# Second block of a two-block transformer kernel: norm weight in the rounding pass, deviation at the PSUM reads, last panels finished tile by tile

## The chip, the cores and the metric

One core of a Trainium2 chip runs the whole program. The metric is the device time of one execution in microseconds, the median of several runs; smaller is better. Before the change the median is 3257.94 us over three runs (3250.87 to 3266.14).

## What is computed

The reference chains two blocks of two layers each over 256 tokens and 1024 channels. The change touches the second block alone:

```
for l in range(DEPTH):                                   # 2 layers
    x = x + 0.5 * swiglu(rmsnorm(x, ffn1_norm[l]), gate, up, down)   # 1024 -> 2816 -> 1024
    h = rmsnorm(x, mix_norm[l])
    proj = h @ w_in[l]          # queries, keys, values, gates of two attention branches
    ...                         # sparse attention, gated linear attention, gated merge
    x = x + y @ w_out[l]
    x = x + 0.5 * swiglu(rmsnorm(x, ffn2_norm[l]), gate, up, down)
return rmsnorm(x, final_norm)

def rmsnorm(x, g):  return x * rsqrt(mean(x * x) + EPS) * g
def swiglu(x, ...): return (silu(x @ w_gate) * (x @ w_up)) @ w_down
```

The deviation of a norm is one number for each token and the weight one number for each channel, so the deviation can be applied before or after a projection, and the weight only before it. All is float32; a product is made of two rounded halves on either side (high and low), three passes of TensorE for one float32 product.

## The kernel before

The residual stream is `y`, transposed: eight tiles of 128 channels by 256 tokens in SBUF. Weights come as panels of 1 MB (128 x 2048 float32) into a ring of four slots. Each panel passes three engines before TensorE may use it: SyncE issues its load once the panel three places ahead in use has begun (`slot`, `panel_begun`), ScalarE rounds it to the high half (`split`, L1466), and GpSimd subtracts to get the low half, in four operations of 128 x 512 (L1446). ScalarE's program has its `split()` calls written into the stream of its other work, two panels ahead of TensorE's use, so that whatever stands before a split delays it.

TensorE (`block.tensor`) works through a panel with 48 matmuls. `abreast` interleaves several outputs, one pass each in turn; `products` finishes one output after the other. Outputs are PSUM banks, taken in turn from eight (`bank`), and each must be read (`bank_read`) before it is taken again.

`rms` stands between two stages. VectorE adds the eight results of the down projection to `y` (L2412) or those of `w_out` (L2640); ScalarE squares the tiles (L1791); TensorE sums the squares over channels by products with ones (L767, 16 matmuls); ScalarE takes the root (L1797); VectorE takes the reciprocal (L2371), multiplies each tile by norm weight and deviation into `plain2` (L2380, twice for the last norm as L2375); ScalarE rounds it to the high half `h2[0]` (L1802), VectorE subtracts to the low half `h2[1]` (L2384, `h_ready`), and TensorE starts on the next panel, a k tile at a time.

`ffn` is eleven pairs of an up and a gate panel, each panel giving two tiles. ScalarE reads the gate tiles with Silu (L1812), VectorE multiplies with the up tiles (L2400) and halves the product (`parts`, L2389 and L2391). Eleven down panels follow, two k tiles each, with all eight outputs abreast, so that the eight results are complete together. `in_projections` is the first part of the mixer: two panels of queries (ScalarE reads them, L1830), two of keys and values that VectorE turns into blocks (L2428), one of 16 columns (`rank`), one of 24, and then keys, values, compression weights and more, among them three small loads (`small_in`) that SyncE issues behind the panel that waits for `rank` to begin. `merge` ends with the four panels of `w_out`.

Between the blocks SyncE waits for the first block's last norm (`y_ready`, L725) before it loads a table of 1 MB, a mask, and then the panels of ffn1. ScalarE takes the two splits of the first panels of a layer behind the squares (`rms(split_first=True)`), not in the stage ahead. At the end the normed tiles are transposed (L810), copied by ScalarE, and stored by one DMA (L734).

The layers of the second block are a loop on all engines. In the first block's MLP of layer 1 the last two panels' splits are left out (L1758), since the next two panels aren't there.

## Time and profile before

| | |
|---|---|
| median of 3 runs | 3257.94 us |
| profiled execution | 3254.99 us, span 3253.2 us, mean granted TensorE clock 0.947 |
| TensorE busy | 2943.5 us (90%) |
| TensorE weight loads | 2605.7 us (80%) |
| GpSimd busy | 1784.8 us (55%) |
| ScalarE busy | 1244.7 us (38%) |
| VectorE busy | 889.1 us (27%) |
| DMA | 422.6 MB, 130 GB/s over the span |

The page is one execution as the hardware profiler saw it. Busy time is that of an engine's instructions and not of the whole path. "PE" is TensorE, "PEld" its weight loads, "DVE" VectorE, "ACT" ScalarE, "POOL" GpSimd, "SP" SyncE. What ended a wait stands in the chain of waits and in the brackets of the timeline; the chain follows the last instruction back to what released it. The second block runs from about 1773 us to the end.

### The profile page before, as it was taken

The page shows a single profiled execution, that of the slowest core. Times are in us where ns is not written, and L with a number is a line of the kernel's source. Part 1 is how long each engine was busy: PE and PEld are TensorE (multiplying, and loading weights), DVE is VectorE, ACT ScalarE, POOL GpSimd, SP SyncE. Part 2 cuts the span into 40 slices and gives each one's busy share as a digit, 9 for nine tenths or more (in the row PEclk, how much of TensorE's full clock was granted, in tenths as well). Part 3 has the DMA queues.
Part 4 walks back from the last instruction along what each step waited for, and adds up shares of the span by engine and source line. Part 5 has one row for each costly group of instructions (what it writes and reads, how often), then busy time and mean ns, then how long its engine had stood idle before and what let it go on. Part 6 is the DMA issues. An engine that isn't in the chain of part 4 may idle for free.

```text
span 3253.2 us, 49328 instructions
## 1 busy us (share of the span) xinstructions
PE 2943.5 (90%) x20273; PEld 2605.7 (80%) x20273; DVE 889.1 (27%) x1620; ACT 1244.7 (38%) x1672; POOL 1784.8 (55%) x1380
## 2 busy tenths in 40 slices
PE   5799888887999979889897999899998999899998
PEld 4576656674887847679897999889998998889998
DVE  1223233125112252333334212144211212144211
ACT  1423443223223233553443434454433434455432
POOL 1220214341545404247585887855887887756885
PEclk8889999989999989999999999999999999999999
DMA  7433325341322313135443556533454556534453
GB/s 222 116 92 112 95 98 156 122 129 30 100 90 91 97 32 91 53 104 156 130 170 128 161 176 169 169 117 117 156 182 156 169 180 171 169 104 130 156 181 117
DMA packets 397385, 422.60 MB, mean 130 GB/s; under 512 B 74550, under 2 KB 367406, under 8 KB 396919
## 3 DMA queue, kind: packets, MB, share of 16 engines
q1 hardware_dynamic: 397208, 420.06, 41.5%
q8 instruction: 134, 2.20, 0.3%
q14 instruction: 43, 0.35, 0.0%
HBM read 418.96 MB, written 3.16 MB: 130 GB/s over the span
## 4 chain that ended last, share of the span: by engine, by line
PE 82%; DVE 5%; POOL 5%; DMA 3%; ACT 3%; issue 2%; SPq 1%; DVEq 0%; POOLq 0%; ACTq 0%
PE ps L783 64%; PE ps L767 16%; POOL ring_r L1446 5%; PE ps L810 2%; ACT ring_hi L1466 1%; DVE arena L2092 1%; DMA ring<-in_w_in 1%; DVE stat L2205 1%; DMA ring<-in_w_ada 1%; DVE arena L2219 1%; DMA arena<-in_bucket_of_block 0%; PE ps L824 0%; DVE arena L2371 0%; DMA ring<-in_ffn_w_gate 0%; DMA ring<-in_w_branch_gla 0%
## 5 line engine op out<-in xcount | busy, mean ns | idle before, releaser
L1446 POOL TENSOR_TENSOR ring_r<-ring,ring_hi 128x512 fp32r<-128x512 f32 x1376 | 1784.6, 1333 | 1439.0 <-ACT ring_hi L1466 1437.0
L783 PE MATMUL ps<-hT_r,ring_hi 128*128 128x256 f32 (+1 forms) x6304 | 1178.7, 310 | 101.5 <-DVE hT_r L2384 36.6
L783 PEld LDWEIGHTS ps<-hT_r,ring_hi 128*128 128x128 f32 x6304 | 956.3, 197 | 169.3 <-issue 44.5
L1466 ACT ACTIVATE ring_hi<-ring 128x2048 fp32r<-128x2048 f32 x344 | 658.0, 1914 | 568.8 <-DMA ring<-in_ffn_w_down 136.3
L783 PE MATMUL ps<-hT_r,ring_r 128*128 128x256 f32 (+1 forms) x3152 | 712.6, 308 | 0.0
L783 PE MATMUL ps<-arena_r,ring_hi 128*128 128x256 f32 (+1 forms) x3792 | 641.8, 311 | 27.0 <-DVE arena_r L2293 9.5
L783 PEld LDWEIGHTS ps<-arena_r,ring_hi 128*128 128x128 f32 x3792 | 542.1, 190 | 74.1 <-issue 23.8
L783 PEld LDWEIGHTS ps<-hT_r,ring_r 128*128 128x128 f32 x3152 | 523.9, 196 | 24.7
L783 PE MATMUL ps<-arena_r,ring_r 128*128 128x256 f32 (+1 forms) x1896 | 358.4, 310 | 0.0
L783 PEld LDWEIGHTS ps<-arena_r,ring_r 128*128 128x128 f32 x1896 | 284.2, 190 | 20.8
L767 PE MATMUL ps<-arena 128*64 128x128 f32 (+9 forms) x1616 | 201.0, 366 | 24.6 <-DVE arena L2181 11.9
L767 PEld LDWEIGHTS ps<-arena 128*64 128x64 f32 (+4 forms) x1616 | 125.8, 174 | 70.4 <-issue 51.4
L2400 DVE TENSOR_TENSOR arena<-arena,ps 128x256 f32 (+1 forms) x88 | 33.1, 418 | 420.9 <-ACT arena L1812 420.9
L767 PE MATMUL ps<-arena,const 128*128 128x256 f32 (+3 forms) x348 | 105.3, 458 | 35.1 <-ACT arena L1494 17.1
L2350 DVE TENSOR_TENSOR arena_r<-arena,arena_r 128x512 fp32r<-128x512 f32 (+1 forms) x64 | 84.3, 1340 | 161.1 <-ACT arena_r L1755 161.1
L810 PE MATMUL ps<-const,arena 128*128 128x128 f32 x480 | 75.9, 307 | 53.8 <-DVE arena L2219 39.2
L767 PEld LDWEIGHTS ps<-arena,const 128*128 128x128 f32 (+2 forms) x348 | 66.1, 200 | 70.7 <-issue 47.4
L767 PE MATMUL ps<-ring_hi,hT_r 128*128 128x128 f32 (+2 forms) x640 | 114.6, 279 | 4.1 <-POOL ring_r L1446 2.5
L810 PEld LDWEIGHTS ps<-const,arena 128*128 128x128 f32 x480 | 63.1, 159 | 68.4 <-DVE arena L2219 50.7
L1632 ACT ACTIVATE arena<-ps,stat,rstd 128x512 f32<-128x512 f32 (+1 forms) x96 | 67.0, 702 | 123.3 <-DVE stat L2209 123.3
L1812 ACT ACTIVATE arena<-ps 128x256 f32<-128x256 f32 x88 | 29.1, 383 | 182.9 <-PE ps L783 182.9
L767 PEld LDWEIGHTS ps<-ring_hi,hT_r 128*128 128x128 f32 (+1 forms) x640 | 93.2, 175 | 6.0 <-POOL ring_r L1446 3.1
(215 smaller groups left out, 1954.7 us busy)
## 6 DMA issues: line engine op xcount, KB each, us to landing
ring<-in_w_in SPq DMA_DIRECT2D x82, 1024.0 KB
ring<-in_w SPq DMA_DIRECT2D x64, 1024.0 KB
ring<-in_w_ada SPq DMA_DIRECT2D x48, 1024.0 KB
ring<-in_ffn_w_up SPq DMA_DIRECT2D x44, 1024.0 KB
ring<-in_ffn_w_gate SPq DMA_DIRECT2D x44, 1024.0 KB
ring<-in_ffn_w_down SPq DMA_DIRECT2D x44, 1024.0 KB
ring<-in_w_in SPq DMA_DIRECT2D x48, 256.0 KB
ring<-in_w_o SPq DMA_DIRECT2D x8, 1024.0 KB
```

What stands on the lines that cost most here:

```text
L767: mm = pe.matmul(o, lhsT, rhs, start=start and j == 0, stop=stop and j == len(passes) - 1, skip_group_check=True)
L783: last[t] = pe.matmul(o, lhsT, rhs, start=start and j == 0, stop=stop and j == n - 1, skip_group_check=True)
L810: return pe.transpose(o, src, ident)
L1446: ins = pool.tensor_tensor(k.ring_lo[s][:, part], k.ring[s][:, part], k.ring_hi[s][:, part], ALU.subtract)
L1466: act.activation(k.ring_hi[s][:, :], k.ring[s][:, :], ACT.Copy).then_inc(k.hi_ready[s], 1)
L1632: act.activation(prob[:, buf, a, 0:n], ps[:, b, 0:n], ACT.Exp, bias=k.stat[:, 8 * buf + a:8 * buf + a + 1], scale=rstd_cq[:, tt:tt + 1] if ...
L1812: act.activation(area(SILU2, 2, 2, SEQ)[:, j % 2, m, :], ps[:, b, 0:SEQ], ACT.Silu).then_inc(k.bank_read[b], 1)
L2092: dve.reciprocal(std, std).then_inc(S["dve_step"], 1)
L2205: ins = dve.tensor_reduce(nmax[:, a:a + 1], ps[:, b, 0:n], AX, ALU.max, negate=True)
L2219: ins = dve.tensor_scalar(p, p, rsum[:, a:a + 1], None, ALU.mult)
L2350: dve.tensor_tensor(hid_lo[:, kt, :], hid[:, kt, :], hid_hi[:, kt % HID_SLOTS, :], ALU.subtract) \
L2400: dve.tensor_tensor(x[:, m, :], area(SILU2, 2, 2, SEQ)[:, j % 2, m, :], ps[:, b, 0:SEQ], ALU.mult) \
```

## The change

- `rms` is gone. ScalarE's `rounded` rounds `y` times norm weight straight to the high half (Identity with a scale for each channel) and squares the same tile behind it; VectorE's `remainders` make the low half from `y`, weight and high half in one operation. For the mixer these halves lie in a buffer of their own, `hq_split`.
- TensorE's `normed_panel` takes the first panel on them, and sums the squares after the fifth k tile (`kt == KD // 2`). ScalarE's `deviation` takes the root, VectorE's `inverted` the reciprocal `rstd2`.
- The deviation is applied where results are read: VectorE reads all four tiles of an ffn pair with a multiplication by `rstd2`, ScalarE applies Silu in SBUF, VectorE multiplies, ScalarE rounds (before, VectorE did), VectorE subtracts. The query tiles are read by VectorE with the deviation. The rest of `in_projections` still takes normed halves `h2`, which are now made behind the first panel.
- The last down panel, and the last panel of `w_out`, are worked one output after the other; residuals, roundings and remainders follow tile by tile. In the merge ScalarE's four splits stand between the roundings.
- SyncE no longer waits for `y_ready`. The two splits of a layer's first panels are taken in the stage ahead (first block's MLP, or the down stage of layer 0).
- The last norm's tiles are transposed without the deviation, its squares are summed to one column for each token, and ScalarE and VectorE apply it in the copies; two stores of 512 KB take the place of one.
- ScalarE's and VectorE's programs have the two layers written out; TensorE and SyncE keep the loop. GpSimd's four operations for a panel stay as they are.

```diff
@@ sync
-            sp.wait_ge(S["y_ready"], KD)
...
-            sp.wait_ge(S["out_ready"], 4)
-            sp.dma_start(out[0].rearrange("(t p) d -> p t d", p=P), area(0, 2, D)).then_inc(S["out_done"], 16)
-            sp.wait_ge(S["out_done"], 16)
+            for t, rows_ready in enumerate(("first_rows", "last_rows")):
+                sp.wait_ge(S[rows_ready], 2)
+                sp.dma_start(out[0, t * P:t * P + P, :], area(0, 2, D)[:, t, :]).then_inc(S["out_done"], 16)
+            sp.wait_ge(S["out_done"], 32)
@@ tensor
-            def rms():
+            def normed_panel(x):
+                w = view(panel(), 0, KD, 256)
                 sq = area(SQ2, KD, SEQ)
-                b = bank()
+                bs, total = [bank() for _ in range(2)], bank()
                 for kt in range(KD):
-                    pe.wait_ge(S["squared"], T.next("squared"))
-                    mm = products(ps[:, b, 0:SEQ], [(ones, sq[:, kt, :])], kt == 0, kt == KD - 1)
-                mm.then_inc(k.bank_done[b], 1)
+                    pe.wait_ge(S["h_ready"], T.next("h_ready"))
+                    mms = abreast([ps[:, b, 0:SEQ] for b in bs],
+                                  [tile(w, m, x, ALL)[kt:kt + 1] for m in range(2)], kt == 0, kt == KD - 1)
+                    if kt == KD // 2:
+                        for j in range(KD):
+                            pe.wait_ge(S["squared"], T.next("squared"))
+                            mm = products(ps[:, total, 0:SEQ], [(ones, sq[:, j, :])], j == 0, j == KD - 1)
+                        mm.then_inc(k.bank_done[total], 1)
+                for b, mm in zip(bs, mms):
+                    mm.then_inc(k.bank_done[b], 1)
...
-                    mms = abreast([ps[:, b, 0:SEQ] for b in bs],
-                                  [[(cut(w, ALL, kt % 2, slice(m * P, m * P + P)), cut(act2_split, ALL, kt, ALL))]
-                                   for m in range(KD)], kt == 0, kt == FT - 1)
-                    if kt == FT - 1:
-                        for b, mm in zip(bs, mms):
-                            mm.then_inc(k.bank_done[b], 1)
+                    if kt < FT - 2:
+                        abreast([ps[:, b, 0:SEQ] for b in bs],
+                                [[(cut(w, ALL, kt % 2, slice(m * P, m * P + P)), cut(act2_split, ALL, kt, ALL))]
+                                 for m in range(KD)], kt == 0, False)
+                for m, b in enumerate(bs):
+                    products(ps[:, b, 0:SEQ], [(cut(w, ALL, j, slice(m * P, m * P + P)), cut(act2_split, ALL, FT - 2 + j, ALL))
+                                               for j in range(2)], False).then_inc(k.bank_done[b], 1)
...
             def in_projections():
+                normed_panel(hq_split)
+                w = view(panel(), 0, KD, 256)
+                two_results(SEQ, [tile(w, m, hq_split, ALL) for m in range(2)])
...
+                        if sem == "merged" and j == 3:
+                            for m, b in enumerate(bs):
+                                products(ps[:, b, 0:SEQ], tile(w, m, x_split, ALL)).then_inc(k.bank_done[b], 1)
+                            continue
...
-            rms()
-            pe.wait_ge(S["final_ready"], T.next("final_ready"))
+            sq = area(SQ2, KD, SEQ)
+            bs, total = [bank() for _ in range(4)], bank()
+            for kt in range(KD):
+                pe.wait_ge(S["final_ready"], T.next("final_ready"))
+                for t in range(2):
+                    at = slice(t * P, t * P + P)
+                    mm = flip(ps[:, bs[2 * (kt // 4) + t], kt % 4 * P:kt % 4 * P + P], plain2[:, kt, at])
+                    if kt % 4 == 3:
+                        mm.then_inc(k.bank_done[bs[2 * (kt // 4) + t]], 1)
+            pe.wait_ge(S["squared"], T.next("squared", KD))
             for t in range(2):
...
+                mm = products(ps[:, total, t:t + 1], [(sq[:, kt, t * P:t * P + P], ones[:, 0:1]) for kt in range(KD)])
+            mm.then_inc(k.bank_done[total], 1)
@@ scalar
-                    if kt % 2 == 1 and (l == 0 or kt < 4 * KD - 4):
+                    if kt % 2 == 1:
                         split()
...
+            def rounded(gain, hi, ready="h_rounded", tiles=None):
                 for kt in range(KD):
-                    b = (T.bank + kt) % BANKS
-                    act.wait_ge(k.bank_read[b], T.value(f"bank{b}"))
+                    if tiles is None:
+                        b = (T.bank + kt) % BANKS
+                        act.wait_ge(k.bank_read[b], T.value(f"bank{b}"))
+                    else:
+                        if kt % 2 == 0:
+                            split()
+                        act.wait_ge(*k.moved(tiles[kt]))
+                    act.activation(hi[:, kt, :], y[:, kt, :], ACT.Identity, scale=gain(kt)).then_inc(S[ready], 1)
                     act.activation(area(SQ2, KD, SEQ)[:, kt, :], y[:, kt, :], ACT.Square).then_inc(S["squared"], 1)
...
+            def ffn(panels_after):
+                def pair(j, two, first=False):
                     split()
                     skip(2)
+                    if first:
+                        deviation()
                     split()
...
+                    skip(2)
+                    s = area(SILU2, 2, 2, SEQ)[:, j % 2]
+                    act.wait_ge(*k.moved(T.last()))
+                    act.activation(s, s, ACT.Silu).then_inc(S["silu_ready"], 1)
+                    act.wait_ge(S["act2_plain"], T.next("act2_plain"))
+                    act.activation(act2_split[0][:, two, :], act2[:, two, :], ACT.Copy).then_inc(S["act2_rounded"], 1)
...
             def in_projections():
...
+                split()
+                skip(2)
+                deviation()
+                skip(2)
+                for kt in range(KD):
+                    act.wait_ge(S["h_plain"], T.next("h_plain"))
+                    act.activation(k.h2[0][:, kt, :], plain2[:, kt, :], ACT.Copy).then_inc(S["h_rounded"], 1)
+                split()
                 for _ in range(2):
                     split()
                     skip(2)
...
+            bs, (b, v) = [T.take() for _ in range(4)], T.take()
+            act.wait_ge(k.bank_done[b], v)
+            act.activation(k.stat[:, 0:2], ps[:, b, 0:2], ACT.Sqrt, scale=1.0 / D, bias=eps).then_inc(k.bank_read[b], 1)
@@ vector
+            def remainders(kts, gain, x_split):
+                for kt in kts:
+                    dve.wait_ge(S["h_rounded"], T.next("h_rounded"))
+                    dve.scalar_tensor_tensor(x_split[1][:, kt, :], y[:, kt, :], gain(kt), x_split[0][:, kt, :],
+                                             ALU.mult, ALU.subtract).then_inc(S["h_ready"], 1)
+            def residuals(scale, gain, x_split):
+                for m in range(KD):
+                    b, v = T.take()
+                    dve.wait_ge(k.bank_done[b], v)
+                    dve.scalar_tensor_tensor(y[:, m, :], ps[:, b, 0:SEQ], scale, y[:, m, :], ALU.mult, ALU.add) \
+                        .then_inc(k.bank_read[b], 1)
+                    if gain and m >= 1:
+                        remainders((m - 1,), gain, x_split)
+                if gain:
+                    remainders((KD - 1,), gain, x_split)
...
+                def pair(j, two, first=False):
+                    up = [T.take() for _ in range(2)]
+                    if first:
+                        inverted()
+                    x, s = act2[:, two, :], area(SILU2, 2, 2, SEQ)[:, j % 2]
+                    for o, tiles in ((x, up), (s, [T.take() for _ in range(2)])):
+                        for m, (b, v) in enumerate(tiles):
+                            dve.wait_ge(k.bank_done[b], v)
+                            ins = dve.tensor_tensor(o[:, m, :], ps[:, b, 0:SEQ], rstd2, ALU.mult).then_inc(k.bank_read[b], 1)
+                    dve.wait_ge(S["silu_ready"], T.next("silu_ready"))
+                    dve.tensor_tensor(x, x, s, ALU.mult).then_inc(S["act2_plain"], 1)
+                    dve.wait_ge(S["act2_rounded"], T.next("act2_rounded"))
+                    dve.tensor_tensor(act2_split[1][:, two, :], x, act2_split[0][:, two, :], ALU.subtract) \
+                        .then_inc(S["act2_split"], 1)
...
+                queries_of = [T.take() for _ in range(2)]
+                inverted()
+                queries_of += [T.take() for _ in range(2)]
...
+                for m, (b, v) in enumerate(queries_of):
                     dve.wait_ge(k.bank_done[b], v)
...
+                    dve.scalar_tensor_tensor(qa[:, m, :], ps[:, b, 0:SEQ], HD ** -0.5, rstd2, ALU.mult, ALU.mult) \
                         .then_inc(k.bank_read[b], 1)
```

## Rows read from the trace of the kernel before

**Rows 1.** The page's chain that ended last: share of the span by engine.

```profile
PE 82%; DVE 5%; POOL 5%; DMA 3%; ACT 3%; issue 2%; SPq 1%; DVEq 0%; POOLq 0%; ACTq 0%
```

**Rows 2.** Chain in order of time, second block: start us, length us, what, matmuls.

```profile
1795.29 129.54 PE ps L783 x1055
1926.58 61.90 PE ps L783 x521
...
2289.49 17.20 PE ps L783 x144
...
2314.32 129.47 PE ps L783 x1055
2445.16 61.93 PE ps L783 x521
```

**Rows 3.** Timeline of norm B: start us, busy us, engine, line, operation [idle before].

```profile
1988.50 2.74 DVE L2412 SCALAR_TENSOR_TENSOR xT<-ps,xT 128x256 f32<-128x256 f32 x8 [60.98 <-PE ps L783]
...
1988.96 2.73 ACT L1791 ACTIVATE arena<-xT 128x256 f32<-128x256 f32 x8 [2.35 <-DVE xT L2412]
...
1989.43 3.72 PE L767 MATMUL ps<-arena,const 128*128 128x256 f32 x16
...
1991.71 1.28 ACT L1797 ACT_TABLE_LOAD   x1
...
1993.69 1.75 DVE L2371 RECIPROCAL arena<-arena 128x256 f32<-128x256 f32 x1 [2.45 <-ACT arena L1797]
...
1997.38 1.22 PE L783 MATMUL ps<-hT_r,ring_hi 128*128 128x256 f32 x4 [4.23 <-DVE hT_r L2384]
```

**Rows 4.** Timeline of TensorE behind norm B, groups of four matmuls.

```profile
1998.83 1.05 PE L783 MATMUL ps<-hT_r,ring_hi 128*128 128x256 f32 x4
...
2003.45 0.64 PE L783 MATMUL ps<-hT_r,ring_hi 128*128 128x256 f32 x4
```

**Rows 5.** Timeline of ScalarE: gate reads of first pairs behind A, C, D.

```profile
1809.66 0.66 ACT L1812 ACTIVATE arena<-ps 128x256 f32<-128x256 f32 x2 [5.00 <-PE ps L783]
...
1810.20 1.92 ACT L1466 ACTIVATE ring_hi<-ring 128x2048 fp32r<-128x2048 f32 x1
...
2328.60 0.66 ACT L1812 ACTIVATE arena<-ps 128x256 f32<-128x256 f32 x2 [5.21 <-PE ps L783]
...
2537.12 0.66 ACT L1812 ACTIVATE arena<-ps 128x256 f32<-128x256 f32 x2 [4.92 <-PE ps L783]
```

**Rows 6.** Timeline of ScalarE and GpSimd around norm B: panels' splits.

```profile
1984.69 1.92 ACT L1466 ACTIVATE ring_hi<-ring 128x2048 fp32r<-128x2048 f32 x1 [3.66 <-DMA ring<-in_w_in]
...
2001.01 1.89 ACT L1466 ACTIVATE ring_hi<-ring 128x2048 fp32r<-128x2048 f32 x1
...
1986.69 5.01 POOL L1446 TENSOR_TENSOR ring_r<-ring,ring_hi 128x512 fp32r<-128x512 f32 x4 [0.53 <-ACT ring_hi L1466]
...
2013.99 16.31 POOL L1446 TENSOR_TENSOR ring_r<-ring,ring_hi 128x512 fp32r<-128x512 f32 x12 [0.70 <-ACT ring_hi L1466]
```

**Rows 7.** Timeline: VectorE and ScalarE operations on SBUF, alone and beside GpSimd.

```profile
1735.63 2.75 DVE L2350 TENSOR_TENSOR arena_r<-arena,arena_r 128x256 fp32r<-128x256 f32 x2 [2.97 <-ACT arena_r L1755]
...
1811.39 0.69 DVE L2391 TENSOR_TENSOR arena_r<-arena,arena_r 128x512 fp32r<-128x512 f32 x1
...
2266.28 1.03 DVE L2632 TENSOR_TENSOR arena<-arena,xT 128x512 f32<-128x512 f32 x1
...
2267.35 0.63 ACT L2003 ACTIVATE arena_r<-arena 128x512 fp32r<-128x512 f32 x1 [3.19 <-DVE arena L2632]
```

**Rows 8.** Timeline of SyncE's queue: first load behind its wait for the norm.

```profile
1773.19 0.38 SPq L726 DMA_DIRECT2D hT<-bias_copies  x1
```

**Rows 9.** Timeline of the program's end.

```profile
3235.10 3.69 PE L767 MATMUL ps<-arena,const 128*128 128x256 f32 x16 [0.23 <-ACT arena L1791]
...
3244.44 3.68 PE L810 MATMUL ps<-const,arena 128*128 128x128 f32 x16 [5.64 <-DVE arena L2375]
...
3248.78 0.39 SPq L734 DMA_DIRECT2D out<-arena  x1
```

More of the change, by code:

```diff
@@ new lines, in ffn @@
+            def ffn(gain, x_split):
+                def pair(j, two, first=False):
[12 more added lines that the diff above has]
+                        .then_inc(S["act2_split"], 1)
+                pair(0, slice(0, 2), first=True)
+                with dve.Fori(0, 5) as i, T.loop(i, 5, {"tiles": 8, "silu_ready": 2, "act2_rounded": 2}):
+                    for j in range(2):
+                        pair(j + 1, bass.ds(i * 4 + (2 + 2 * j), 2))
+                residuals(0.5, gain, x_split)
```

195 lines of the change are left out of this document (64 added, 131 removed).

## Prediction, made before the change was run

> **What bounds the kernel now.** I read the chain of waits first, then the chain in order of time for the second block, then the timelines of single stretches. TensorE carries 82% of the chain [rows 1]; the rest sits in short stretches where another engine ends the wait, so an edit is worth only what it takes out of TensorE's own line. The second block is a few long runs of matmuls with holes between them [rows 2]. Inside the runs nothing but TensorE counts: 144 matmuls take 17.20 us, so a weight panel (48 matmuls) takes 5.76 us and a k tile of two outputs (6 matmuls) 0.72 us. The holes lie where a norm stands between two stages, eight times: before ffn1 of layer 0 (A), before the two mixers (B, E), before the two ffn2 (C, F), before ffn1 of layer 1 (D), and at the end (G); a smaller one lies at the start of each of the four down projections.
>
> B shows what a hole is made of [rows 3]. The down projection ends about 1989.3. Residuals (8 in 2.74 us) and squares follow, TensorE sums the squares in 3.72 us, ScalarE loads its table and takes the root, the reciprocal takes 1.75, and the first matmul starts at 1997.38: 8.1 us with 3.7 of work. Then the clock: four matmuls take 1.05 us right after the hole, 0.64 us five microseconds later [rows 4], that is 1.2 against 2.4 GHz after an idle stretch of 4.23 us. C shows the price: from 2314.32 to the ScalarE read at 2328.60 [rows 5] there are two panels, 14.3 us where 11.5 are due, 2.8 us lost.
>
> **The change part by part.** I count from the end of the stage in front (0) to the end of the second panel behind it. In the changed order the first panel needs no deviation, and the sum of squares lies inside it: 5.76 + 3.72 = 9.5, second panel at 15.2, if the operands arrive in time.
>
> C and F. Before: w_out ends at 2289.49 + 17.20 = 2306.7, the second panel at 2328.6, so 22.0 us. After: six of eight residuals come from earlier panels, and only the last two are young; each needs a ScalarE pass and a VectorE remainder, and TensorE asks for them after four k tiles and the sums. Nothing late: 15.2. Gain 6.8 each, 13.6. The splits of w_out's later panels now queue on ScalarE behind the roundings of two tiles (4 passes of 0.34 = 1.4 us); GpSimd has that much room, since it was busy with the panel ahead anyway. Cost 0, at most 2 each.
>
> D. Before: down ends 2445.16 + 61.93 + 0.8 = 2507.9, second panel 2537.1, so 29.2 us; this hole is longer because the two splits of the next panels came after the norm. After: they are taken in the down stage. The operands are tighter. ScalarE is in a split until -2.7 and GpSimd works from -2.6 to 2.4 (B's own rows, the same stage) [rows 6]. A VectorE operation with two SBUF inputs took 1.37 us beside GpSimd (2.75 for two) [rows 7] against an estimated 0.42 alone (0.69 for twice the width), while those with a PSUM input kept 0.34 [rows 3]. So of eight remainders three cost 1.37 and five 0.42, with eight residuals of 0.34 between: operands at -0.9, 0.9, 2.6, 3.3, 4.1, and the last near 6. TensorE loses 1.2 us in the first three k tiles and none later, because the sums (3.72 us) stand ahead of tile 5. 16.4 us; gain 12.8. Bounds: no collision 14.0; all eight at 1.37 about 10.5.
>
> A. y is complete at 1773.2, where SyncE's wait ends [rows 8]. Before, the second panel ended at 1809.6 [rows 5]. After: table load, first rounding and remainder (1.28 + 0.34 + 0.42), with VectorE's memsets of the second block in front of the remainder, bring the first operand by an estimated 1776.2. TensorE has idled, so the first 5 to 6 us run at half clock (+2.8): 1776.2 + 15.2 + 2.8 = 1794.2. Gain 15.4. This needs both panels loaded and split before the norm ends: without SyncE's wait on y the loads go out during the MLP, one table of 1 MB ahead of them, and ScalarE splits inside the MLP. The table's 1 MB now shares the queue with the last w2 panel; a panel has some 3.9 us of room in such a stage (below, in the pairs), less than a table of a panel's size would take alone. I take 0, at most 2.
>
> B and E. Here the gain is taken back. The first hole closes as in D, and the first panel ends near 10.7. But the plain norm for the rest of the projection comes later: ScalarE finishes rounding (6.0), splits the third panel (7.9), loads its table and takes the root (9.7), reciprocal to 11.5. Then sixteen VectorE operations with eight ScalarE roundings; the first two collide with GpSimd, the rest go at the pace of before, where rounding ended 5.5 us after its start: 18.4. The split of the fourth panel is queued behind these roundings, so 20.3, and GpSimd delivers at 25.4, while TensorE wants it at 22: it waits 3 to 4 us and may fall to the lower clock again (2.8). GpSimd's next three panels take 16.3 [rows 6] and end at 25.4 + 16.3 = 41.7; before they ended at 2013.99 + 16.31 = 2030.3, which is 41.0. From there the mixer hangs on that stream. Gain 0; bounds: 6.7 each (all of it kept) and -3.
>
> The Trainium skill ("ScalarE: Activation LUTs", section "What ACT_TABLE_LOAD costs") adds a drain of about 1.38 us to each load of 1.28. The trace shows no such drain: squares end at 1988.96 + 2.73 = 1991.69, the load starts at 1991.71 [rows 3]. By the page B and E would lose 1.4 us more each, and the sum would be 3209.
>
> Down starts. ScalarE read the gate tiles first and VectorE multiplied after; TensorE waited from 1795.29 + 129.54 = 1924.8 to 1926.58 [rows 2]. Now VectorE alone reads: two reads of 0.37, so 0.9 after the end instead of 1.75. Gain 0.85 in each of four, 3.4.
>
> G. Before, the end of the last down (about 3234.9, where the sums start [rows 9]) to the end of the span took 18.3: sums, root, reciprocal, eight scalings, 16 transposes of 0.23 each (3.68 us), the copy, the store issued at 3248.78 and 4.4 to the end. After: transposes start with 0, end by 3.7; 16 one-column products for the sums at no more than the 0.23 of a transpose, 7.4; root, reciprocal of two columns 0.5; two copies of 0.6; store 4.4: 13.5. Gain 4.8; bounds 3 to 6.
>
> Inside the pairs. This is the one cost that could repeat 40 times. Let T be the end of a gate panel. Before, ScalarE read two tiles and began the next split at T + 0.6 [rows 5]; with 1.92 for it and 5.0 for GpSimd the panel was there at T + 7.6, and TensorE wants it at T + 11.5: 3.9 us of room. Now ahead of that split stand two VectorE reads (0.75), Silu on 512 columns (0.63, the nearest ScalarE row), the product (0.69 alone, 1.03 beside GpSimd) and the rounding (0.63) [rows 7], with an estimated 0.07 for each of four handovers (from product to rounding the rows show 2267.35 - 2267.31 = 0.04): the split begins near T + 3.3. 2.7 of 3.9 us are used up, 1.2 are left. Cost 0.
>
> **Sum.** 13.6 + 12.8 + 15.4 + 0 + 3.4 + 4.8 = 50.0 us. The profiled execution took 3255.0 (span 3253.2), so 3205; the median of the runs shown is 3 us above the profiled one, and I say 3206.
>
> **The rivals.**
> Crowding (3222): where holes close, GpSimd loses the pauses in which it caught up, and VectorE's remainders meet it more often. For it: in the merge its operations stand nearly end to end, and the colliding row is three times its lone price. Against: it needs 5.0 to 5.4 us for a panel against TensorE's 5.76. Price: C and F gain 3 less each, D 3.5 less, A 2, B and E lose 2 each: 16 us. The Trainium skill ("GPSIMD Engine Reference", section "Specifications") says VectorE shares its SBUF interface with GpSimd for operations of two SBUF inputs, which the rows bear out.
>
> B and E keep what they gain (3193): if GpSimd's stream isn't what the mixer hangs on, or rounding ends earlier than 18.4. For it: later panels also wait for a small load that is issued with the fifth panel. Price 13 us in the other direction.
>
> Slower (about 3295): the chain in the pairs. Each microsecond by which the split begins after T + 4.5 stalls TensorE in each of 40 pairs, 40 us. From T + 5.75 all of the gain is gone; at T + 6.7 it is 90 - 50 = 40 slower. That would take product, Silu and rounding of twice their rows each. Against: no row of this width is above 1.03.
>
> The change doesn't do it (3245): the holes stay, since the operands come late and the sums' place in the panel doesn't hide it; only A's loads and G remain.
>
> **How the numbers follow.** Forecast 3206 with 0.62, crowding 0.18, B and E kept 0.10, holes stay 0.04, slower 0.06. The range goes from 3190 (a part of B and E kept) to 3230 (crowding, with its bounds): it leaves out the slower case, the holes, and a little below. 0.5% of this kernel is 16 us, about what a measurement tells from no change. Faster by more: the first three, 0.90; within: 0.04, the holes; slower by more: 0.06.
>
> **What would show it.** Right: TensorE's rows run on from the last down or w_out panel without a gap over 1 us and without 1.05 us groups at C, D and F; 16 sums stand inside the first panel; at B a hole of 3 to 4 us ahead of the fourth panel, ended by GpSimd, and the mixer no earlier; in the pairs the split begins near T + 3.3 and TensorE waits for nothing. Wrong: TensorE waiting on GpSimd's ring operations in the pairs (the slower rival); ffn spans longer than 129.5 + 61.9; remainders of 1.37 in all eight at C.

## The result and the profile after

The changed kernel took 3205.7 us (median of 4 runs, 3204.7 to 3211.7) against 3260.8 us (4 runs) of the kernel before on the same chip: ratio 0.9838, interval 0.9811 to 0.9866. The forecast was 3206. That the median meets it within a microsecond is luck: two more measurements of the same kernel gave 3209.1 and 3204.2. The profiled execution has a span of 3204.4 us against 3253.2.

The page of the changed kernel: busy time, then the chain by engine (to be laid beside [rows 1]).

```profile
PE 2932.3 (92%) x20289; PEld 2595.3 (81%) x20289; DVE 976.8 (30%) x1694; ACT 1270.8 (40%) x1683; POOL 1812.4 (57%) x1380
...
PE 81%; DVE 6%; POOL 6%; ACT 3%; DMA 3%; issue 1%; SPq 1%; DVEq 0%; POOLq 0%; ACTq 0%
```

The chain by engine hardly moved: what went out of it were idle stretches of TensorE that it had booked on several engines. They are seen in the chain in order of time (start, length, what), which answers to [rows 2]:

```profile
1787.99 123.00 PE ps L779 x1025
1911.92 51.48 PE ps L779 x433
...
2298.80 123.19 PE ps L779 x1025
2422.91 51.49 PE ps L779 x433
```

From the first long run (A) to the next one of that length (C) it was 2314.32 - 1795.29 = 519.0 us and is 2298.80 - 1787.99 = 510.8. The run itself has its old pace of 0.12 us for a matmul (1025 instead of 1055, since the sums cut off the first 30; 433 instead of 521, since the last products stand under another line).

Norm B in the changed kernel, timeline of TensorE, ScalarE, VectorE and GpSimd, beside [rows 3] and [rows 6]:

```profile
1978.00 0.74 PE L779 MATMUL ps<-arena_r,ring_hi 128*128 128x256 f32 x4 [0.46 <-DVE arena_r L2387]
1979.54 3.62 PE L763 MATMUL ps<-arena,const 128*128 128x256 f32 x16
1999.46 0.73 PE L779 MATMUL ps<-hT_r,ring_hi 128*128 128x256 f32 x4 [2.75 <-POOL ring_r L1448]
...
1983.69 0.47 ACT L1809 ACTIVATE arena<-ps,const 128x256 f32<-128x256 f32 x1
1986.54 0.42 ACT L1841 ACTIVATE hT_r<-arena 128x256 fp32r<-128x256 f32 x1 [2.37 <-DVE arena L2443]
1992.36 3.70 ACT L1468 ACTIVATE ring_hi<-ring 128x2048 fp32r<-128x2048 f32 x2
...
1984.20 1.75 DVE L2405 RECIPROCAL arena<-arena 128x256 f32<-128x256 f32 x1 [3.41 <-ACT arena L1809]
1985.99 2.35 DVE L2443 SCALAR_TENSOR_TENSOR arena<-xT,vecT,arena 128x256 f32<-128x256 f32 x3
...
1994.34 25.86 POOL L1448 TENSOR_TENSOR ring_r<-ring,ring_hi 128x512 fp32r<-128x512 f32 x19 [6.68 <-ACT ring_hi L1468]
```

The hole of 4.23 us in front of the first matmul is gone (two gaps of 0.46 are left), but ScalarE's split of the fourth panel stands behind eight roundings, GpSimd idles 6.68 us, and TensorE waits 2.75 us for GpSimd: the hole was moved.

Stage by stage, before and after, each from the end of the stage in front to the end of the second panel behind it (B and E: to the end of the mixer):

| place | before | after | gain | forecast |
|---|---|---|---|---|
| A (from the start of the first block's last sums) | 53.2 | 36.8 | 16.4 | 15.4 |
| B, E (whole mixers) | 317.3, 316.8 | 317.3, 316.9 | 0 | 0 |
| C, F | 22.0, 22.0 | 14.8, 14.8 | 14.3 | 13.6 |
| D | 29.2 | 17.4 | 11.8 | 12.8 |
| four pairs-and-down stretches | 179.7, 179.3, 179.7, 179.4 | 178.7, 178.9, 178.7, 178.9 | 3.0 | 3.4 |
| G, down end to end of span | 18.3 | 12.35 | 6.0 | 4.8 |
| first block | | 2.5 later | -2.5 | 0 |

Together 51.4 - 2.5 = 48.9, and 3253.2 - 3204.4 = 48.8. The 2.5 us of the first block are there in its first 110 us and constant from then on; nothing of the code in those 110 us was changed.

### The profile page after: what moved, and what is told of

Read it like the earlier page. It is cut to its first block, busy times and chain, and to the rows that moved or that the text cites. A ratio compares the mean times of both kernels' runs of the same rounds, so it can differ in the third digit from the quotient of the medians.

```text
span 3204.4 us, 49071 instructions
## 1 busy us (share of the span) xinstructions
PE 2932.3 (92%) x20289; PEld 2595.3 (81%) x20289; DVE 976.8 (30%) x1694; ACT 1270.8 (40%) x1683; POOL 1812.4 (57%) x1380
## 3 DMA queue, kind: packets, MB, share of 16 engines
q1 hardware_dynamic: 397224, 420.06, 42.2%
## 4 chain that ended last, share of the span: by engine, by line
PE 81%; DVE 6%; POOL 6%; ACT 3%; DMA 3%; issue 1%; SPq 1%; DVEq 0%; POOLq 0%; ACTq 0%
PE ps L779 61%; PE ps L763 17%; POOL ring_r L1448 6%; PE ps L806 2%; ACT ring_hi L1468 1%; DMA ring<-in_w_in 1%; DVE arena L2104 1%; DVE stat L2217 1%; DMA ring<-in_w_ada 1%; DVE arena L2231 1%; PE ps L820 0%; DMA arena<-in_bucket_of_block 0%; DMA ring<-in_w_branch_gla 0%; DVE arena_r L2387 0%; DVE arena L2443 0%
## 5 line engine op out<-in xcount | busy, mean ns | idle before, releaser
L1448 POOL TENSOR_TENSOR ring_r<-ring,ring_hi 128x512 fp32r<-128x512 f32 x1376 | 1812.2, 1354 | 1369.0 <-ACT ring_hi L1468 1367.6
L779 PE MATMUL ps<-hT_r,ring_hi 128*128 128x256 f32 (+1 forms) x6176 | 1149.3, 309 | 83.2 <-POOL ring_r L1448 40.6
L779 PEld LDWEIGHTS ps<-hT_r,ring_hi 128*128 128x128 f32 x6176 | 929.2, 195 | 149.8 <-issue 50.4
L779 PE MATMUL ps<-hT_r,ring_r 128*128 128x256 f32 (+1 forms) x3088 | 695.1, 306 | 0.0
L779 PEld LDWEIGHTS ps<-arena_r,ring_hi 128*128 128x128 f32 x3728 | 535.1, 190 | 74.5 <-issue 24.2
L779 PEld LDWEIGHTS ps<-hT_r,ring_r 128*128 128x128 f32 x3088 | 509.0, 194 | 24.7
L763 PEld LDWEIGHTS ps<-arena 128*64 128x64 f32 (+4 forms) x1616 | 126.1, 174 | 70.4 <-issue 51.4
L2423 DVE TENSOR_TENSOR arena<-ps,arena 128x256 f32<-128x256 f32 (+1 forms) x176 | 66.5, 419 | 270.8 <-PE ps L779 270.6
L763 PE MATMUL ps<-arena,const 128*128 128x256 f32 (+3 forms) x332 | 98.6, 450 | 18.4 <-ACT arena L1496 16.8
L1821 ACT ACTIVATE arena<-arena 128x512 f32<-128x512 f32 x44 | 27.8, 632 | 209.8 <-DVE arena L2423 209.8
L2353 DVE TENSOR_TENSOR arena<-arena,ps 128x512 f32 (+3 forms) x64 | 32.6, 550 | 223.5 <-ACT arena L1747 223.5
```

Of the source, the lines that this page charges most:

```text
L763: mm = pe.matmul(o, lhsT, rhs, start=start and j == 0, stop=stop and j == len(passes) - 1, skip_group_check=True)
L779: last[t] = pe.matmul(o, lhsT, rhs, start=start and j == 0, stop=stop and j == n - 1, skip_group_check=True)
L1448: ins = pool.tensor_tensor(k.ring_lo[s][:, part], k.ring[s][:, part], k.ring_hi[s][:, part], ALU.subtract)
L2353: dve.tensor_tensor(o, relu(l, j), ps[:, b, 0:n], ALU.mult).then_inc(k.bank_read[b], 1)
L2423: ins = dve.tensor_tensor(o[:, m, :], ps[:, b, 0:SEQ], rstd2, ALU.mult).then_inc(k.bank_read[b], 1)
```

## A yardstick: the second block by itself

The first block is the same code in all kernels below but pool_long (the last two splits of its last MLP apart), yet it doesn't take the same time. The reciprocal of its last norm marks its end; timeline of VectorE, in this order before, the changed kernel, and two more executions of the changed kernel ("again" and "3"):

```profile
1765.97 1.75 DVE L2092 RECIPROCAL arena<-arena 128x256 f32<-128x256 f32 x1 [2.48 <-ACT arena L1498]
...
1768.44 1.75 DVE L2104 RECIPROCAL arena<-arena 128x256 f32<-128x256 f32 x1 [2.48 <-ACT arena L1500]
...
1777.07 1.75 DVE L2104 RECIPROCAL arena<-arena 128x256 f32<-128x256 f32 x1 [2.49 <-ACT arena L1500]
...
1766.06 1.75 DVE L2104 RECIPROCAL arena<-arena 128x256 f32<-128x256 f32 x1 [2.48 <-ACT arena L1500]
```

Up to 11 us between executions of one program. So I cut each trace at this reciprocal and at those of the six norms behind it, and compare stretches. "ffn" is the sum of the four stretches that hold a feed-forward part (A to B, C to D, D to E, F to the end), "mixers" B to C and E to F.

| kernel | first block ends | to norm A | ffn | mixers | second block | ratio to before (interval) |
|---|---|---|---|---|---|---|
| before | 1766.0 | 23.2 | 830.4 | 633.6 | 1487.2 | |
| changed | 1768.4 | 20.1 | 786.1 | 629.8 | 1436.0 | 0.9838 (0.9811 to 0.9866) |
| changed, again | 1777.1 | 20.1 | 786.6 | 629.1 | 1435.7 | 0.9844 (0.9824 to 0.9863) |
| changed, 3 | 1766.1 | 20.1 | 785.7 | 627.8 | 1433.6 | 0.9859 (0.9839 to 0.9879) |
| ahead_only | 1771.0 | 13.8 | 823.7 | 632.6 | 1470.1 | 0.9946 (0.9924 to 0.9967) |
| abreast_again | 1781.4 | 20.1 | 794.3 | 625.4 | 1439.8 | 0.9864 (0.9839 to 0.9889) |
| split_early | 1772.2 | 20.1 | 788.1 | 627.8 | 1436.0 | 0.9851 (0.9828 to 0.9874) |
| pe_unrolled | 1776.7 | 20.2 | 783.2 | 626.5 | 1429.8 | 0.9823 (0.9807 to 0.9840) |
| pe_unrolled_2 | 1766.4 | 20.1 | 784.2 | 628.3 | 1432.6 | 0.9846 (0.9829 to 0.9863) |
| chain_1 | 1766.3 | 20.1 | 790.3 | 629.8 | 1440.2 | 0.9853 (0.9830 to 0.9875) |
| chain_4 | 1766.5 | 20.1 | 813.4 | 630.1 | 1463.6 | 0.9933 (0.9912 to 0.9955) |
| chain_7 | 1772.6 | 20.1 | 875.6 | 625.9 | 1521.6 | one run, 3296.0 us |
| pool_long | 1795.0 | 19.9 | 818.8 | 631.5 | 1470.1 | 1.0037 (1.0019 to 1.0054) |

Three executions of the changed kernel agree within 0.9 us in "ffn", within 2 in "mixers" and within 2.4 in the second block, where their whole spans differ by 13. abreast_again, chain_1, chain_4 and pool_long ran on another chip than the changed kernel's repetitions; the last column compares each with the kernel before on its own chip, where the medians of before lay within 3253 and 3261. (The norm's reciprocal now comes inside the first panel, so a row compares changed kernels among each other exactly, and with before only in the sum.)

## Experiments

**The change once more**, to know the scatter.

> The changed kernel once more, unchanged, as the yardstick for the other runs on this chip. Expected: ratio to the kernel before 0.984, in the profile the same stages as in its first profile within 0.5 us; the first 110 us may differ by 2 to 3 us from execution to execution.

3209.1 us, ratio 0.9844. The extra 8 us of the profiled execution lie ahead of the second block.

**Only the early loads and splits, on the kernel before.**

```diff
-            sp.wait_ge(S["y_ready"], KD)
...
-                    if kt % 2 == 1 and (l == 0 or kt < 4 * KD - 4):
+                    if kt % 2 == 1:
...
-            with act.Fori(0, LAYERS) as l, T.loop(l, LAYERS, PER_LAYER["act"]):
-                rms(split_first=True)
+            for l in range(LAYERS):
+                rms()
...
-                ffn(ahead=False)
+                ffn(ahead=l + 1 < LAYERS)
```

> The kernel before with one part of the change alone: no wait of SyncE for y, and the two splits of a layer's first panels taken in the stage ahead; ScalarE's layer loop is written out for that. Expected from the profile of before: A's norm loses the two splits and the loads, its first matmul comes at about 1789 instead of 1795 (6.6 us), D's hole shrinks from 29.2 to about 22 us (7), together 13.6 us of the 50, about 3241 where before is 3255. Rival (the loads and splits are what matters at A and D, the form of the norm little): 25 us or more.

3240.4 us; the second block became 17.1 us shorter. 13.1 of it lie between the first block's end and norm B (23.2 + 204.5 became 13.8 + 200.9), that is at A, where I had expected 6.6, and 3.1 at D, where I had expected 7: the two misses go opposite ways and the sum came out near the 13.6. So a third of the 51 us is worth having without touching the arithmetic. A's 16.4 us are mostly this; the other 34 belong to the rest of the change together.

**The last panels abreast again**, not output by output.

```diff
-                    if kt < FT - 2:
-                        abreast(... kt == 0, False)
-                for m, b in enumerate(bs):
-                    products(... FT - 2 + j ..., False)
+                    mms = abreast(... kt == 0, kt == FT - 1)
...
-                        if sem == "merged" and j == 3:
```

> The changed kernel with the last down panel and the last panel of w_out worked abreast again, all outputs complete together; residuals, roundings and remainders stay as they are. Theory (ScalarE needs 0.71 us for a tile's rounding and square, so eight tiles take 5.7 us, and tile by tile hides five of them beside TensorE): G about 4.7 us later, D 2, each mixer 2.7 because its third panel's split comes later, C and F 0.3: 12 us slower in all (8 to 16). Rival (the sum of squares inside the first panel hides it anyway): under 3 us.

"ffn" is 8.2 us longer than in the changed kernel; the mixers came out 4.4 shorter, of which their own scatter covers 2, so the second block shows only 3.8 and the ratio can't tell it. The mixer between norms B and C is 5.0 us shorter: TensorE was busy 290.33 us in it at a granted clock of 0.97 (293.54 at 0.96 in the changed kernel). What gave the rest stays open. The cost lies where residuals come all at once: F to the end +4.2, A to B +2.0, D to E +1.9; C to D shows 0.1, probably since the loop's end (below) hides it there. TensorE at the end of this kernel:

```profile
3206.08 0.87 PE L806 MATMUL ps<-const,arena 128*128 128x128 f32 x6 [1.22 <-DVE xT L2390]
```

The transposes go at ScalarE's pace (a rounding and a square for each tile), in the changed kernel they run in one row (below). The 4.2 us at the end of the program are the part that nothing behind it can give back. The tile by tile order is worth between 3.8 (the second block) and 8.2 us ("ffn") here, less than the 12 expected; the cut at a reciprocal counts as "ffn" what the next mixer may take back.

**The fourth panel's split ahead of the roundings** (B, E).

```diff
                 skip(2)
+                split()
                 for kt in range(KD):
...
-                split()
```

> ScalarE's split of the mixer's fourth panel stands ahead of the eight roundings instead of behind them, in the time in which ScalarE waits for the reciprocal. Theory (the mixers gain nothing because this split is queued behind the roundings, and GpSimd's stream sets the mixer's pace afterwards): GpSimd gets the fourth panel about 6 us sooner, but then meets VectorE's sixteen operations, which go from 0.7 us for a k tile to up to 2.4; the fifth panel's split comes no sooner, so each mixer gains about 1 us, 2 us in all (0 to 4). Rival (the split order is all there is): the wait of 3 to 4 us ahead of the fourth panel goes in both mixers with its lower clock, 7 to 13 us in all.

No gain: 3210.5 us, second block 1436.0, mixers 627.8 within the scatter. The trace shows why. First VectorE of this kernel behind norm B, then TensorE:

```profile
1989.95 3.42 DVE L2443 SCALAR_TENSOR_TENSOR arena<-xT,vecT,arena 128x256 f32<-128x256 f32 x3
1993.29 1.51 DVE L2447 TENSOR_TENSOR hT_r<-arena,hT_r 128x256 fp32r<-128x256 f32 x1
1997.96 0.41 DVE L2447 TENSOR_TENSOR hT_r<-arena,hT_r 128x256 fp32r<-128x256 f32 x1
...
1997.70 0.74 PE L779 MATMUL ps<-hT_r,ring_hi 128*128 128x256 f32 x4 [1.86 <-DVE hT_r L2447]
1999.59 1.05 PE L779 MATMUL ps<-hT_r,ring_hi 128*128 128x256 f32 x4
2016.85 1.96 PE L763 MATMUL ps<-arena,const 16*128 16x256 f32 x8 [0.69 <-DMA const<-in_cmp_v_w]
```

GpSimd now runs while VectorE makes the normed halves, and operations of 0.41 us take 1.51 beside it. The wait of 2.75 us for GpSimd became one of 1.86 for VectorE, and behind it TensorE's clock fell here (four matmuls in 1.05 us; granted clock 0.54 from 1998.5 to 2002.1), which it did not behind the 2.75 us: four k tiles took 4.45 us where 2.88 is the pace, so some 1.5 us of the gain went there. The matmul of the last row stands 28.69 us behind norm B's reciprocal (1988.16), in the changed kernel 28.77 (2012.97 - 1984.20): what the fourth panel won was gone two steps later, and there a small load comes next in line. So B and E hang on several things that are late by about the same; the forecast named one of them, GpSimd's stream.

**TensorE's layer loop written out.**

```diff
-            with pe.Fori(0, LAYERS) as l, T.loop(l, LAYERS, PER_LAYER):
+            for l in range(LAYERS):
```

> TensorE's layer loop written out, nothing else. Theory (the 2.1 us before the first matmul of layer 1 are the loop's end on TensorE's sequencer, since three operands were ready by then): the gap at D goes, 2.1 us faster, and no other stage moves. Rival (my prediction's reading: colliding remainders hold the first k tiles at D): the gap stays, time unchanged.

At D the changed kernel and the one written out, timeline of TensorE from the last down product:

```profile
2485.36 0.28 PE L763 MATMUL ps<-arena_r,ring_r 128*128 128x256 f32 x1
2487.75 0.73 PE L779 MATMUL ps<-hT_r,ring_hi 128*128 128x256 f32 x4 [2.12 <-DVE hT_r L2387]
```

```profile
2483.17 0.28 PE L763 MATMUL ps<-arena_r,ring_r 128*128 128x256 f32 x1
2483.28 0.64 PE L779 MATMUL ps<-hT_r,ring_hi 128*128 128x256 f32 x4
...
2485.61 0.75 PE L779 MATMUL ps<-hT_r,ring_hi 128*128 128x256 f32 x4
```

(The second fence is of pe_unrolled_2, the repetition below.) The trace puts the wait of 2.12 us down to VectorE's remainders, but the first three were done at 2483.3, 2484.8 and 2486.2; without the loop TensorE runs on at once and loses 0.17 us in the fourth k tile (2485.20 + 0.24 is where it was due). The wait was the loop's. It is 2.1 to 2.5 us in all nine traces of a changed kernel that keeps the loop. The same edit once more, with more runs, and the changed kernel beside it:

> The changed kernel with TensorE's loop over the layers written out. In the trace of its first run the wait of 2.1 to 2.5 us at the start of layer 1 was gone, and 0.7 us at the end of the program; another 3 us of its second block came from a granted clock that was higher in one mixer. Theory: 2.8 us faster than the changed kernel, ratio to it 0.999. Rival: the 3 us of clock come back in each run, 6 us, 0.998.

> The changed kernel once more, beside the one with the loop written out, to see what the loop is worth in the median: 3 us more than that one, and 0.984 to 0.985 of the kernel before. Its second block, from the reciprocal of the first block's last norm to the end, 1436 us in the trace, whatever the first block takes.

C to D takes 194.5 and 194.6 written out, 196.3 to 196.5 with the loop: 1.9 us, in both. The other microseconds of the first trace were scatter: the 0.7 us at the end of the program came and went in both kernels (sums to reciprocal 5.51 or 6.2), and the mixers differ by the clock. For 2384 matmuls from norm B to norm C TensorE was busy 293.50 us in one execution and 290.86 in the other. Medians 3202.0 and 3203.5 against 3209.1 and 3204.2: written out is not slower, and the 2 us are less than medians can tell here; the traces show them.

**The chain in the pairs made longer** by ScalarE copies of 128x512 (0.55 us each) in front of the rounding.

```diff
                     act.wait_ge(S["act2_plain"], T.next("act2_plain"))
+                    for _ in range(N):
+                        act.activation(area(14336 + 512 * _, 2, SEQ), act2[:, two, :], ACT.Copy)
                     act.activation(act2_split[0][:, two, :], act2[:, two, :], ACT.Copy)...
```

> One more ScalarE copy of 128x512 into unused space ahead of the rounding, in each of the 44 pairs: 0.53 us more in the chain from the end of a gate panel to the next split. Theory (0.9 us of room left, 1818.8 against 1817.9 in the profile of after): nothing, under 1 us but where the stage's ends show it. Rival (the chain is already what bounds the pairs): 20 us slower.

> Four more such copies in each pair, about 2.2 us in the chain. Theory (0.9 us of room): 1.3 us of stall in each of 40 pairs, 50 us slower, so that the whole gain of the change is gone; TensorE waits on GpSimd's ring operations in the pairs. Rival (the ring's other panels give the room back): under 10 us.

One copy: no wait of TensorE for GpSimd is listed in the pairs; "ffn" +4.2 us, 2.0 of it at D, where this execution fell to the slow clock behind the loop's end (groups of 1.05 us), and 0.6 to 1.0 in each other stretch. Most of these are waits too short to be listed: at two panels of each stretch (in the first at 1816.73 and 1863.16) the matmuls' starts stand up to 0.4 us apart instead of 0.12, 0.55 to 0.8 us a stretch, and the splits in front of the two began 4.3 and 4.4 us after the gate reads. Four copies: +27.4 us, half of the price that I had set. GpSimd and one pair of the other engines in this kernel (T is the start of the gate reads, 1829.29):

```profile
1812.29 10.51 POOL L1448 TENSOR_TENSOR ring_r<-ring,ring_hi 128x512 fp32r<-128x512 f32 x8 [1.08 <-ACT ring_hi L1468]
1825.12 10.51 POOL L1448 TENSOR_TENSOR ring_r<-ring,ring_hi 128x512 fp32r<-128x512 f32 x8 [2.32 <-ACT ring_hi L1468]
1836.70 10.52 POOL L1448 TENSOR_TENSOR ring_r<-ring,ring_hi 128x512 fp32r<-128x512 f32 x8 [1.06 <-ACT ring_hi L1468]
...
1829.29 0.76 DVE L2425 TENSOR_TENSOR arena<-ps,arena 128x256 f32<-128x256 f32 x2 [4.55 <-PE ps L779]
1834.72 3.70 ACT L1468 ACTIVATE ring_hi<-ring 128x2048 fp32r<-128x2048 f32 x2
1830.21 0.74 PE L779 MATMUL ps<-hT_r,ring_hi 128*128 128x256 f32 x4 [0.84 <-POOL ring_r L1448]
```

The split begins at T + 5.4, its first panel is ready at 1836.70 + 5.26 = T + 12.7, and TensorE asks for it at T + 11.5: 1.2 us late. But the idle times of GpSimd alternate, and TensorE waits 0.84 to 0.86 us in every second pair, four times in this stretch, with two more waits of 0.27 us (the six of the next run's expectation). Two pairs together take 24.4 us instead of 23.0. The wait falls behind the gate reads, so the next pair's chain starts on time while its panel is wanted later: one wait pays for two pairs. I had charged it to each. Seven copies test that:

> The changed kernel with seven extra ScalarE copies of 128x512 ahead of the rounding in each pair of hidden tiles (their results are used by nothing). In the run with four copies (0.55 us each) the split began 5.4 to 5.7 us after the gate reads, GpSimd's idle time between pairs went 1.06, 2.32, 1.06, 2.32 us and TensorE waited in 6 of 12 pairs. Theory formed from that: a wait in one pair gives the next pair that much more room, so that a chain that is late by s us costs s in every second pair. With seven copies the split begins at about T+7.2, 2.9 us beyond the 4.3 us at which the wait would begin: alternate waits of 2.9 us, 16 us in each feed-forward layer half, 64 us in all over the changed kernel's second block. Rival, the price of the prediction: 2.9 us in every pair, about 128 us. Second rival: by the four-copy run's 27.7 us for four copies in proportion, 48 us.

TensorE waited 6 times in the first feed-forward part, 14.9 us together (16 expected). But "ffn" grew by 89.5 us, not 64: after waits of this length the clock can fall.

```profile
1841.39 0.74 PE L779 MATMUL ps<-hT_r,ring_hi 128*128 128x256 f32 x4 [3.24 <-POOL ring_r L1448]
1842.24 1.06 PE L779 MATMUL ps<-hT_r,ring_hi 128*128 128x256 f32 x4
1846.57 0.64 PE L779 MATMUL ps<-hT_r,ring_hi 128*128 128x256 f32 x4
```

1.06 us for four matmuls and then 0.64, 1.2 and 2.4 GHz. The granted clock of this stretch (1800 to 2004) is 0.95, in the four-copy kernel (1794 to 1979) 1.00, whose waits were 0.84. So the price per microsecond rises: half of it in each pair as long as the waits are short (27.4 us for 1.2 us in 44 pairs), and the clock on top when they are longer (89.5 for 2.9). The shortest wait with slow groups behind it was 1.80 us here, and some longer ones, of 1.9 to 2.5 us, had none.

**GpSimd's remainder as one operation of 128x2048** in place of four.

```diff
-                    for c0 in range(0, SLOT, SLOT // 4):
+                    for c0 in range(0, SLOT, SLOT):
```

> GpSimd takes a panel in one operation of 128x2048 instead of four of 128x512, in the changed kernel. Theory (a VectorE operation with two SBUF inputs waits for the GpSimd operation that runs, so 1.2 to 1.4 us now, up to 5 then): remainders at the norms, product and subtraction in the pairs and the remainders of the first block's MLP stretch to several us; the first block's MLP needs two of them for a panel of 5.76 us: 100 to 300 us slower. Rival (the two engines share the port element by element): within 1%.

3268.5 us: the whole gain is gone, some 60 us, though neither number that I had set is met. The second block took 34 us more. The first ended 29 us later than in before, 15 of them there by 790 us as in other traces (last section), 14 behind that, in stages where the other kernels' traces keep their distance, so I put them down to the edit. Groups of VectorE in the second block, first of the changed kernel, then of this one (busy us, mean ns):

```profile
L2425 DVE TENSOR_TENSOR arena<-arena 128x512 f32 (+1 forms) x44 | 61.2, 1390 | 30.7 <-ACT arena L1821 30.7
L2387 DVE SCALAR_TENSOR_TENSOR hT_r<-xT,vecT,hT_r 128x256 fp32r<-128x256 f32 x24 | 22.4, 933 | 1.1 <-ACT hT_r L1799 0.9
```

```profile
L2425 DVE TENSOR_TENSOR arena<-arena 128x512 f32 (+1 forms) x44 | 154.7, 3515 | 30.7 <-ACT arena L1821 30.7
L2387 DVE SCALAR_TENSOR_TENSOR hT_r<-xT,vecT,hT_r 128x256 fp32r<-128x256 f32 x24 | 44.7, 1864 | 3.0 <-ACT hT_r L1799 3.0
L2423 DVE TENSOR_TENSOR arena<-ps,arena 128x256 f32<-128x256 f32 (+1 forms) x176 | 66.4, 418 | 213.5 <-PE ps L779 213.2
```

The product, with two SBUF inputs, waits until GpSimd's operation in progress is over, here 4.6 us long; the reads with a PSUM input keep 0.42. One pair of this kernel, VectorE and GpSimd:

```profile
1858.17 3.45 DVE L2425 TENSOR_TENSOR arena<-arena 128x512 f32 x1 [0.70 <-ACT arena L1821]
1851.85 9.22 POOL L1448 TENSOR_TENSOR ring_r<-ring,ring_hi 128x2048 fp32r<-128x2048 f32 x2 [3.29 <-ACT ring_hi L1468]
```

GpSimd's two operations end at 1861.07; the product ends at 1861.62, 0.55 later. So it is in all eleven pairs of this stretch but the first, where GpSimd is idle and the product takes 0.69 us, and the same 0.55 us stand behind GpSimd's short operations in the changed kernel: the product waits for the end of one operation, whatever its length. From the fifth pair on it takes 4.2 to 4.4 us and the split begins at T + 6.4 to T + 6.6, later than in chain_4, but GpSimd needs 0.6 us less for a panel, and the cost is of a like size (32.7 against 27.4 us). This is the slower rival's mechanism at half its price: it is the shortness of GpSimd's four operations that keeps it away. GpSimd itself would gain (1597.3 / 344 = 4.64 us for a panel against 1812.2 / 344 = 5.27), which helps nobody.

## Why the prediction was right, and which terms were not

- **C and F, 6.8 each.** Measured 7.15 and 7.1. The sums cost 3.46 us of TensorE's time, not the 3.72 of [rows 3]: the length of a row holds the end of the last matmul too, which the next k tile overlaps (3.62 us with it; the granted clock was 1.00 in both). The operands came in time, as the step said; no row of over 0.5 us idle.
- **D, 12.8.** Measured 11.8, and the term for its loss was right in size by accident. I gave 1.2 us to collisions of remainders with GpSimd; four remainders did collide (1.15 to 1.23 each, not three at 1.37), and with the loop written out they cost 0.17. The 2.1 us came from the loop's end on TensorE, which stood in the trace of before as an idle time for which nothing was waited ("issue"), in a row that I had not costed:

```profile
2511.68 5.25 PE L767 MATMUL ps<-arena,const 128*128 128x256 f32 x16 [3.77 <-issue]
```

At B, where no loop ends, the same collisions did cost what was forecast: the first five k tiles took 5.07 us (1974.47 to 1979.54), at C 3.60.
- **A, 15.4.** Measured 16.4. TensorE started at 1778.58, where 1776.2 + 2.5 (the drift) was forecast, but two steps in front of it were off and cancelled: no table load stands ahead of the first rounding (1775.62), and VectorE's memsets in front of the first remainder took 2.2 us (1775.86 to 1778.04). The microsecond more is the sums (3.46 for 3.72) and the slow clock, which cost 2.2 us, not 2.8.
- **B and E, 0.** The number is right, and TensorE waits where it was said, on GpSimd ahead of the fourth panel (2.75 us; 3 to 4 forecast). GpSimd's stream of that panel and the next three ends 40.9 us behind the down end, 41.0 before. Wrong is that this stream alone decides. In the kernel before TensorE waited at this point for a small load; in the changed kernel it waits 0.51 us for GpSimd and then runs slowly. TensorE before, then changed:

```profile
2029.65 1.96 PE L767 MATMUL ps<-arena,const 16*128 16x256 f32 x8 [1.16 <-DMA const<-in_cmp_v_w]
2032.00 0.40 PE L767 MATMUL ps<-hT_r,ring_hi 128*128 128x256 f32 x2
...
2015.46 0.80 PE L763 MATMUL ps<-hT_r,ring_hi 128*128 128x256 f32 x2 [0.51 <-POOL ring_r L1448]
2016.27 0.63 PE L763 MATMUL ps<-hT_r,ring_hi 128*128 128x256 f32 x2
```

The 24 matmuls that begin here began 42.2 us behind the down end before (2031.54) and 41.0 now, but took 2.98 us before and take 4.46 now; the granted clock is 0.62 from 2015.5 to 2019.9, and was 1.00. So 1.2 us were kept up to here and lost to the clock: that exactly nothing is left is partly luck. ScalarE needed 0.71 to 0.73 us for a tile's rounding and square (two times 0.34 forecast), VectorE's three plain operations collided (2.35 us), and the fourth split began at 17.9 where 18.4 was forecast.
- **The drain of a table load.** Norm B once more shows none; by the Trainium skill ("ScalarE: Activation LUTs", section "What ACT_TABLE_LOAD costs") B and E would have lost more, and this the trace doesn't bear out: the load of 1.28 us begins at 1982.40, when ScalarE's split ends (1980.49 + 1.89 = 1982.38), and the root follows at 1983.69.
- **Down starts, 3.4.** Measured 3.0: TensorE idles 0.82 us instead of 1.64 at two of them, and gained 0.5 at each of the two others, where it had idled 1.28.
- **G, 4.8.** Measured 6.0. A transpose took 0.12 us where I had 0.23: the row of before stood at half the clock (granted 0.50 from 3244.5 to 3248) behind a hole of 5.64 us [rows 9], now TensorE comes straight from the down products (1.00). The sums are 32 one-column matmuls in 4.40 us, where I had 16 in 3.7; transposes and sums together end 6.2 us behind the down end, not 7.4. This fence answers to [rows 9]:

```profile
3192.06 1.91 PE L806 MATMUL ps<-const,arena 128*128 128x128 f32 x16
3193.81 4.40 PE L763 MATMUL ps<-const,arena 128*128 128x1 f32 x32
3198.25 0.26 ACT L2031 ACTIVATE stat<-ps,const 128x2 f32<-128x2 f32 x1 [3.40 <-PE ps L763]
3200.03 0.84 SPq L730 DMA_DIRECT2D out<-arena  x2
```

- **Inside the pairs, 0.** Right. Timeline of a pair; T is the start of the gate reads:

```profile
1807.34 0.76 DVE L2423 TENSOR_TENSOR arena<-ps,arena 128x256 f32<-128x256 f32 x2 [4.87 <-PE ps L779]
1808.79 1.10 DVE L2425 TENSOR_TENSOR arena<-arena 128x512 f32 x1 [0.70 <-ACT arena L1821]
1810.66 1.90 ACT L1468 ACTIVATE ring_hi<-ring 128x2048 fp32r<-128x2048 f32 x1
```

The split begins at T + 3.3 (forecast T + 3.3); in other pairs the product takes 1.7 us and it is T + 3.9. The waits begin by the rows of chain_1 and chain_4 where the split is later than T + 4.3, so 0.3 to 1.0 us of room is left, not 1.2. The price behind it, 40 us for each microsecond, was nearly twice too high for short waits (27.4 us for 1.2) and still too high with the clock's fall on top (89.5 for 2.9).

Of the rivals, crowding didn't come (at a mean product of 1.39 us the pairs kept room), B and E kept nothing, the holes went.

## What to carry to other kernels

Cut each trace at fixed instructions and compare stretches; the scatter of code that wasn't touched was here as large as a third of the effect. Ask of a moved wait what comes next and next again: the fourth panel's split was second in a row of three. A chain beside the bound engine costs nothing until its room is used, then half of its lateness where a wait also delays the next demand, and more once the waits are long enough for the clock to fall; what sets its length can be another engine's grain, as GpSimd's four short operations did.

## What the hardware showed that I had not expected

- A VectorE operation with two SBUF inputs waits for the GpSimd operation in progress to end: the same product took 1.39 us in the mean beside operations of 1.3 us, and 3.5 us beside those of 4.65, up to 4.42; with a PSUM input 0.42 in both. The Trainium skill ("GPSIMD Engine Reference", section "Specifications") tells of the shared interface; the size of the wait is in these runs.
- The end of a hardware loop on TensorE cost 2.1 to 2.5 us of idle time, booked on another engine's semaphore.
- The first block's time depends on small shifts at its start: traces whose first reciprocal (near 87 us) differs by up to 4 us stand 15 us apart at its end, with steps near 486, 770 and 800 us. I didn't find out why.
- TensorE's clock fell (four matmuls in 1.05 us) behind waits of 1.80, 2.52 and 3.24 us in the pairs of chain_7 and of 1.86 us in split_early, not behind 2.75 us at norm B of the changed kernel (behind the same wait at norm E it fell in two of three executions), and never behind the waits of 0.84 in chain_4's pairs. At norm B of all three executions of the changed kernel it fell later, behind a wait of 0.5 us that follows others of 2.75 and 1.92 us. Behind the loop's end at D, an idle of 2.1 to 2.5 us, it fell in two traces (chain_1, split_early) and not in the changed kernel's three: one and the same hole cost 2 us more or nothing.
